# Where four modulation units of each layer are loaded, multiplied and turned

## The chip, the cores and the metric

The kernel runs on one core of one Trainium2 chip. The metric is the device time of one launch in microseconds (us); the times below are medians over runs. The profile and its trace are of one further execution of the same program.

## The reference, cut to what matters

The kernel computes one inference step of a two-layer backbone on 640 tokens (128 context, 512 latent), D_MODEL = 1024, in float32. What matters here is where the modulation vector `mod` is made and where each sixth of it is used:

```python
mod_ctx = (jax.nn.silu(c_ctx) @ w_ada[l] + b_ada[l])[None, None, :]   # w_ada[l]: 1024 x 6144
mod_lat = (jax.nn.silu(c) @ w_ada[l] + b_ada[l])[:, None, :]
...
def trunk_layer(x, mod, p, lam_init, rope, ctx):
    shift_m, scale_m, gate_m, shift_f, scale_f, gate_f = jnp.split(mod, 6, axis=-1)
    h = rms_norm(x, p['norm_mix']) * (1.0 + scale_m) + shift_m
    mix, own_ctx = token_mixers(h, p, lam_init, rope, ctx)
    x = x + gate_m * mix
    h = rms_norm(x, p['norm_ffn']) * (1.0 + scale_f) + shift_f
    x = x + gate_f * conv_ffn(h, p)
    return x, own_ctx
```

`token_mixers` holds three attentions (A differential, B latent, C grouped-query), each projected, gated by a sigmoid of its own 1024 columns of the input projection, summed, and multiplied by `w_o`. `conv_ffn` multiplies by `w_up`, applies a width-3 convolution and a gated product, and multiplies by `w_down`. The last sixth of the modulation, `gate_f`, is first read when the output of `w_down` is added to x.

## The kernel before, in words

Activations lie in SBUF with features on partitions: `xT` (x, eight tiles of 128 features by 640 tokens), and `hhi`/`hlo`, a high and a low part of the normed input. Every float32 weight is also split, on ScalarE into `whi` (line 1443) and on VectorE into `wlo` (line 1765), and every product is three matmuls (high by high, high by low, low by high). Weights arrive in units of 1 MB in `raw`, which has two slots; a split takes half a unit (a sub) and writes one of two sub buffers.

`build_plan()` writes out one list of steps, and every engine walks this same list and emits those steps that concern it. So the order in each engine's queue is the order of the list. `unit` is a load (SyncE's queue, `load_unit`), `split` the two halves of the weight split, `gate_quarter` a quarter of a gate tile's matmuls (line 1169, 12 matmuls), `gate` a whole gate tile (line 1147). `prefetch(ahead)` puts loads and splits into the list ahead of the products that need them. A load into a slot waits until the slot's former content has been used: for ordinary weights until the last split (`lo_ready`), for a modulation unit until its matmuls (`ada_summed`).

A modulation unit is 256 of the 6144 columns of `w_ada`, so a layer has 24. Step `ada` (line 1076) multiplies it straight from its `raw` slot: eight matmuls of 32 output partitions by 256 columns, into the upper half of PSUM bank 6. `ada_row` (VectorE, line 1730) copies the sums to `ada_rows`, and the `ada_turn` of that unit (line 1086: two products of a 128x128 tile with two columns), which the list holds one unit later, adds the four row groups and turns them into feature columns, kept in the low columns of bank 6. All users of bank 6 wait in `bank6_free()` for `pair3_read` (its readers, `ada_row` among them), `sums_read` and `mod_ready`. `mod` (VectorE, lines 1699 and 1703) then adds the bias and forms the scales.

The first eight units of layer 0 are made at the start of the program. The other 16, and the first eight of layer 1, are made in layer 0, four of them around the attention of branch C; in layer 1 the 16 that are left are made, again four around attention C. There the fill of the attention is, in order: one `ada`, eight quarters, one `ada`, eight quarters, two `ada`. `attention()` spreads its fill over 20 cycles by costs (`QUARTER` 1.8, `ADA_COST` 1.4). In a cycle TensorE computes scores of one block of 128 queries (line 1299), transposes the probabilities of the block before (1311) and multiplies the one before that by the values (1338); VectorE takes maxima (1839), reciprocals and products; ScalarE takes exponentials (1575); a new score waits until the exponentials of the one before are done.

After attention C come the last `ada_turn`, `mod`, and `branch(2)`: two gate tiles, four products with `w_branch_c`. Then `ffn()`: four units of `w_o` (step `wo`), the second norm, the `w_up` and `w_down` loops. The second norm is the steps `norm` (ten 128x1 records at line 1103 sum the squares, VectorE reads them at 1734, GpSimd takes the power at 2020, VectorE makes five diagonals at 1689), `spread` (line 1095) and `apply` (ScalarE 1432, VectorE 1748 and 1754). It cannot begin until the last `wo` output has been added to `xT`, squared and summed.

## Time and profile before

| | |
|---|---|
| median of 3 runs | 2800.79 us (2800.14 to 2802.28) |
| profiled execution, its own time | 2795.99 us |
| its span, first to last instruction | 2794.2 us |
| mean granted TensorE clock | 0.956 of full |
| TensorE / VectorE / ScalarE / GpSimd busy | 91% / 50% / 36% / 15% of the span |
| attention C, first score to last values | 699.7 to 807.7 us (layer 0), 2066.8 to 2172.4 us (layer 1) |
| last `w_o` matmul to first `w_up` matmul | 924.8 to 942.9 us (layer 0), 2289.4 to 2307.6 us (layer 1) |

Busy time counts computing instructions only. A stretch in which TensorE idles is read in the timeline: the bracket at the end of a row is the engine's idle time before the row and the instruction that ended it. PEclk is the granted TensorE clock as a share of full speed (2.4 GHz); the records show it at 1.00 or 0.50 (1.2 GHz).

### The profile page before, as it was taken

To read this page: it belongs to the slowest core of one execution; us is meant where nothing else is said; L and a number is where in the kernel's file an instruction comes from. 1 tells how busy PE (TensorE), PEld (TensorE's weight loads), DVE (VectorE), ACT (ScalarE), POOL (GpSimd) and SP (SyncE) were. 2 spreads that over 40 slices of the span, in tenths; PEclk is the share of its full clock that TensorE was granted. 3 is DMA by queue.
4 is the path that set the end of the run, shared out by engine and by line. 5 is a ranking of instruction groups with operands and counts; after the bars stand their busy time and mean duration, and the time that the engine had idled before them with its cause. 6 is when DMAs were issued, how large, how long until landed. Compare 5 with 4: busy or idle time off the path is not lost.

```text
span 2794.2 us, 42894 instructions
## 1 busy us (share of the span) xinstructions
PE 2546.8 (91%) x17075; PEld 2298.6 (82%) x17075; DVE 1399.7 (50%) x2386; ACT 1001.0 (36%) x1721; POOL 405.5 (15%) x362
## 2 busy tenths in 40 slices
PE   6989989988989799999988899898989889999999
PEld 4768976677779799999976688666967789999998
DVE  3665256644645444334445753575357445442453
ACT  4343144423432444123242532453235225421332
POOL 0400030123002022012004000220220201210220
PEclk8999999999999899999999999999999899999999
DMA  6201213322212122232222112222210221222222
GB/s 220 82 25 46 81 62 126 119 71 78 69 46 76 46 75 68 71 85 72 59 77 63 35 61 67 67 76 80 65 61 31 76 76 46 75 72 79 75 59 85
DMA packets 252830, 202.75 MB, mean 73 GB/s; under 512 B 9876, under 2 KB 235910, under 8 KB 252678
## 3 DMA queue, kind: packets, MB, share of 16 engines
q1 hardware_dynamic: 245574, 197.67, 23.2%
q10 hardware_dynamic: 7104, 2.95, 0.4%
q8 instruction: 108, 1.77, 0.3%
q14 instruction: 44, 0.36, 0.0%
HBM read 196.50 MB, written 4.10 MB: 72 GB/s over the span
## 4 chain that ended last, share of the span: by engine, by line
PE 76%; issue 8%; DVE 7%; ACT 6%; POOL 2%; DMA 0%; POOLq 0%; ACTq 0%; DVEq 0%; SPq 0%
PE ps L1147 44%; PE ps L1299 5%; PE ps L1169 5%; PE ps L1311 3%; PE ps L1132 3%; PE ps L1134 3%; PE ps L1133 3%; PE ps L1338 3%; ACT prob L1575 2%; PE ps L1076 1%; PE ps L1242 1%; DVE wlo L1765 1%; PE ps L1259 1%; ACT hf L1432 1%; PE ps L1086 1%
## 5 line engine op out<-in xcount | busy, mean ns | idle before, releaser
L1765 DVE TENSOR_TENSOR wlo<-raw,whi 128x1024 fp32r<-128x1024 f32 (+4 forms) x288 | 359.8, 1250 | 546.1 <-ACT whi L1443 545.3
L1147 PE MATMUL ps<-hhi,whi 128*128 128x320 f32 x2048 | 479.2, 316 | 28.1 <-DVE hlo L1748 13.3
L1147 PE MATMUL ps<-hlo,whi 128*128 128x320 f32 x2048 | 474.4, 313 | 0.0
L1147 PE MATMUL ps<-hhi,wlo 128*128 128x320 f32 x2048 | 473.5, 313 | 0.0
L1443 ACT ACTIVATE whi<-raw 128x1024 fp32r<-128x1024 f32 (+4 forms) x288 | 281.2, 978 | 393.7 <-PE ps L1147 282.5
L1147 PEld LDWEIGHTS ps<-hhi,whi 128*128 128x128 f32 x2048 | 348.6, 192 | 37.9 <-issue 28.4
L1147 PEld LDWEIGHTS ps<-hlo,whi 128*128 128x128 f32 x2048 | 350.0, 192 | 0.0
L1147 PEld LDWEIGHTS ps<-hhi,wlo 128*128 128x128 f32 x2048 | 349.6, 191 | 0.0
L1839 DVE TENSOR_REDUCE negmax<-ps 128x1 f32<-128x640 f32 x192 | 152.1, 821 | 132.6 <-PE ps L1299 132.6
L2040 POOL TENSOR_TENSOR rstd<-smean,mhalf 128x4 f32<-128x4 f32 (+3 forms) x96 | 117.1, 1223 | 612.8 <-DVE smean L1815 612.5
L1132 PE MATMUL ps<-whi,hhi 128*128 128x512 f32 (+2 forms) x480 | 180.7, 376 | 12.2 <-issue 5.7
L1585 ACT ACTIVATE probT<-ps 128x512 f32<-128x512 f32 (+1 forms) x172 | 88.3, 513 | 255.9 <-PE ps L1311 255.9
L1134 PE MATMUL ps<-whi,hlo 128*128 128x512 f32 (+2 forms) x480 | 178.1, 371 | 0.0
L1133 PE MATMUL ps<-wlo,hhi 128*128 128x512 f32 (+2 forms) x480 | 178.0, 371 | 0.0
L2064 POOL TENSOR_TENSOR va<-va,vg 128x640 f32<-128x640 f32 x44 | 74.7, 1698 | 649.8 <-ACT vg L1641 649.8
L1147 PE MATMUL ps<-ahi,whi 128*128 128x320 f32 x704 | 161.2, 310 | 4.5 <-DVE wlo L1765 3.9
L1575 ACT ACTIVATE prob<-ps,negmax 128x640 f32<-128x640 f32 x192 | 150.5, 792 | 34.3 <-DVE negmax L1839 34.1
L1147 PE MATMUL ps<-ahi,wlo 128*128 128x320 f32 x704 | 160.6, 309 | 0.0
L1147 PE MATMUL ps<-alo,whi 128*128 128x320 f32 x704 | 160.5, 309 | 0.0
L1169 PE MATMUL ps<-hhi,whi 128*128 128x320 f32 x384 | 138.2, 360 | 8.5 <-DVE wlo L1765 8.5
L1311 PEld LDWEIGHTS ps<-ident,prob 128*128 128x128 f32 x840 | 91.8, 141 | 58.9 <-issue 24.0
L1311 PE MATMUL ps<-ident,prob 128*128 128x128 f32 x840 | 127.6, 282 | 12.4 <-DVE prob L1870 8.4
(208 smaller groups left out, 4237.9 us busy)
## 6 DMA issues: line engine op xcount, KB each, us to landing
raw<-in_w_up SPq DMA_DIRECT2D x88, 512.0 KB, 4.9
raw<-in_w_in SPq DMA_DIRECT2D x40, 1024.0 KB, 5.2
raw<-in_w_ada SPq DMA_DIRECT2D x40, 1024.0 KB, 5.2
raw<-in_w_down SPq DMA_DIRECT2D x16, 768.0 KB, 4.8
raw<-in_w_down SPq DMA_DIRECT2D x16, 640.0 KB, 4.5
adaw<-in_w_ada SPq DMA_DIRECT2D x8, 1024.0 KB, 10.5
raw<-in_w_o SPq DMA_DIRECT2D x8, 1024.0 KB, 5.1
raw<-in_w_branch_a SPq DMA_DIRECT2D x4, 1024.0 KB, 6.1
```

Of the source, the lines that this page charges most:

```text
L1132: pe.matmul(out, hhi[:, kt, c], wh, start=kt == 0, stop=False)
L1133: pe.matmul(out, hhi[:, kt, c], wl, start=False, stop=False)
L1134: mm = pe.matmul(out, hlo[:, kt, c], wh, start=False, stop=kt == KD - 1)
L1147: mm = pe.matmul(out, w[:, sub, c], m[:, kt, o:o + HALF], start=first and i == 0 and a == 0, stop=last and i == len(ks) - 1 and a == 2)
L1169: mm = pe.matmul(bank(6)[:, OFF:], w[:, s["sub"], c], m[:, kt, o:o + HALF], start=kt == a == 0, stop=kt == KD - 1 and a == 2)
L1299: mm = pe.matmul(out, qt[:, q * P:(q + 1) * P], kt[:, SEQ + c:SEQ + c + HALF], start=True, stop=True)
L1311: mm = pe.transpose(bank(bk)[:, i * P:(i + 1) * P], src, ident[:, :])
L1443: act.activation(dst(whi), src, ACT.Copy).then_inc(S["hi_ready"], 1)
L1575: act.activation(prob[:, slot + m, :], run(m), ACT.Exp, bias=negmax[:, at], accum_out=den[:, at])\
L1765: dve.tensor_tensor(dst(wlo), src, dst(whi).bitcast(F32), ALU.subtract).then_inc(S["lo_ready"], 1)
L1839: dve.tensor_reduce(negmax[:, slot + m:slot + m + 1], run(m), AX.X, ALU.max, negate=True)\
L2040: pool.tensor_tensor(rstd[:, par, 0:heads], smean[:, par, 0:heads], mhalf[:, 0:heads], ALU.pow)\
```

## The change

Units 20 to 23 of each layer, whose 1024 columns are `gate_f`, leave the common row of units. The others are made in the order of a list, `ADA_ORDER`; the fill of attention C is then the 16 quarters alone. The four units get SBUF places of their own: `adaC` over the space of `qC`, `kC` and `vC`, `adaT` behind `gatedC`. Step `load_tail` loads all four in SyncE's queue, behind the load of the first `w_o` unit and ahead of the second. In the second norm, steps `tail` multiply them on TensorE into banks 0 to 3 behind the last `w_o` matmuls and ahead of `norm`; ScalarE copies the sums back over the units' own first columns; `tail_turn` turns them on TensorE between `norm` and `spread`; `tail_mod` adds the bias on VectorE after `apply`. `down_out` gets a wait for `mod_ready`.

```diff
+ADA_TAIL = range(5 * KD // 2, 6 * KD // 2)
+ADA_ORDER = [(l + (u < ADA_FIRST // 2), u) for l in range(DEPTH)
+             for u in [*range(ADA_FIRST // 2, ADA_TAIL[0]), *range(ADA_FIRST // 2 if l + 1 < DEPTH else 0)]]
...
     def queue_ada(n):
         for _ in range(n):
-            of, u = divmod(count["ada_unit"], 3 * KD)
+            of, u = ADA_ORDER[count["ada_unit"]]
...
-                for u in (2, 4):
-                    queue_ada(1)
-                    queue_gates(2, u, 1)
-                queue_ada(2)
+                queue_gates(2, 2, 2)
                 queue_branch(2)
...
-        attention("C", range(NH), [ada_steps, quarter_gates, quarter_gates, ada_steps, quarter_gates, quarter_gates,
-                                   ada_steps, ada_steps],
+        attention("C", range(NH), [quarter_gates] * 4,
...
-        left = fm_units("wo", KD // 2, SUB, [], early=last, between=[dict(step="zero", l=l, what="wo")], l=l)
-        norm2 = [dict(step=x, which=1, l=l) for x in ("norm", "spread")]
-        norm2.append(dict(step="apply", which=1, l=l, ks=range(KD), kept=False))
+        left = fm_units("wo", KD // 2, SUB, [], early=last, between=[dict(step="zero", l=l, what="wo"), dict(step="load_tail", l=l)], l=l)
+        norm2 = [dict(step="tail", l=l, i=i) for i in range(len(ADA_TAIL))] + [dict(step="norm", which=1, l=l)]
+        norm2 += [dict(step="tail_turn", l=l, i=i, c=ada_column(u)) for i, u in enumerate(ADA_TAIL)]
+        norm2 += [dict(step="spread", which=1, l=l), dict(step="apply", which=1, l=l, ks=range(KD), kept=False),
+                  dict(step="tail_mod", l=l)]
...
+                def load_tail(s):
+                    sp.wait_ge(S["av_done"], n("av_done"))
+                    sp.wait_ge(S["lam_step"], n("lam_step"))
+                    sp.wait_ge(S["rows_turned"], n("rows_turned"))
+                    for i, u in enumerate(ADA_TAIL):
+                        sp.dma_start(tail_unit(i).rearrange("p (k c) -> p k c", k=KD),
+                                     w_ada[s["l"]:s["l"] + 1, :, u * 256:(u + 1) * 256].rearrange("l (k p) c -> p (l k) c", p=P))\
+                          .then_inc(S["tail_full"], 16)
...
+                def tail(s):
+                    i = s["i"]
+                    pe.wait_ge(S["tail_full"], n("tail_full"))
+                    pe.wait_ge(S["fm_read"], n("fm_read", -2))
+                    for k in range(KD):
+                        g = 32 * (k % 4)
+                        mm = pe.matmul(bank(i)[g:g + 32, 0:256], cpad[:, k, :], tail_unit(i)[:, k * 256:(k + 1) * 256],
+                                       start=k < 4, stop=k >= 4)
+                    mm.then_inc(S["tail_summed"], 1)
+
+                def tail_turn(s):
+                    bank6_free()
+                    pe.wait_ge(S["tail_read"], n("tail_read", s["i"] + 1 - len(ADA_TAIL)))
+                    for j in range(2):
+                        c = s["c"] + 2 * j
+                        mm = pe.matmul(bank(6)[:, c:c + 2], tail_unit(s["i"])[:, j * P:(j + 1) * P], add4[:, :],
+                                       start=True, stop=True)
+                    mm.then_inc(S["ada_done"], 1)
...
+                def tail(s):
+                    act.wait_ge(S["tail_summed"], n("tail_summed", 1))
+                    act.activation(tail_unit(s["i"])[:, 0:256], bank(s["i"])[:, 0:256], ACT.Copy).then_inc(S["tail_read"], 1)
...
+                def tail_mod(s):
+                    l, t, m = s["l"], 2 * ADA_TAIL[0], 2 * len(ADA_TAIL)
+                    c = ADA_AT + 2 * (t - ADA_FIRST)
+                    dve.wait_ge(S["ada_done"], n("ada_done"))
+                    dve.tensor_tensor(mod[:, l, t:t + m, :], bank(6)[:, c:c + 2 * m].rearrange("p (t j) -> p t j", j=2),
+                                      PT[:, l, t:t + m].unsqueeze(2).to_broadcast([P, m, 2]), ALU.add).then_inc(S["mod_ready"], 1)
...
                 def down_out(s):
                     dve.wait_ge(S["sub_done"], n("sub_done"))
+                    dve.wait_ge(S["mod_ready"], n("mod_ready"))
```

## Rows read from the trace of the kernel before

**Rows 1.** The page: busy us (share of the span) and instructions of each engine.

```profile
PE 2546.8 (91%) x17075; PEld 2298.6 (82%) x17075; DVE 1399.7 (50%) x2386; ACT 1001.0 (36%) x1721; POOL 405.5 (15%) x362
```

**Rows 2.** Windows of layer 0: length, busy us per engine, PEclk, DMA share, GB/s.

```profile
712.00:757.00 45.00, 44.56 (x396) 35.14 (x394) 30.95 (x59) 22.21 (x52) 0.00 (x0) 0.99 0.01 2
...
807.80:820.50 12.70, 3.90 (x24) 2.54 (x24) 4.48 (x10) 4.62 (x6) 0.00 (x0) 0.66 0.43 117
...
924.80:942.90 18.10, 4.73 (x15) 3.41 (x15) 9.21 (x18) 5.36 (x8) 1.17 (x1) 0.59 0.21 58
```

**Rows 3.** Timeline, end of attention C, layer 0 (start us, us, engine line op).

```profile
806.54 0.61 PE L1086 MATMUL ps<-add,ada_rows 128*128 128x2 f32 x4
806.67 0.37 SPq L980 DMA_DIRECT2D raw<-in_w_in  x1
807.08 0.66 PE L1333 MATMUL ps<-probT,vC 128*64 128x128 f32 x8
811.90 2.00 ACT L1443 ACTIVATE whi<-raw 128x1024 fp32r<-128x1024 f32 x2 [6.90 <-DMA raw<-in_w_in]
...
814.13 0.42 DVE L1730 COPY ada_rows<-ps 128x256 f32<-128x256 f32 x1
...
814.81 1.94 PE L1076 MATMUL ps<-raw,cpad 128*32 128x256 f32 x16 [7.07 <-issue]
816.68 1.01 PE L1086 MATMUL ps<-add,ada_rows 128*128 128x2 f32 x4
...
820.56 0.87 PE L1147 MATMUL ps<-hhi,whi 128*128 128x320 f32 x2 [1.27 <-DVE scale L1703]
...
825.49 0.50 PE L1147 MATMUL ps<-hhi,whi 128*128 128x320 f32 x2
```

**Rows 4.** Timeline, start of attention C, layer 0.

```profile
699.66 2.50 PE L1299 MATMUL ps<-kC,qC 64*128 64x320 f32 x8 [0.77 <-ACT PT L1401]
...
706.87 0.42 DVE L1730 COPY ada_rows<-ps 128x256 f32<-128x256 f32 x1
...
707.39 0.60 PE L1169 MATMUL ps<-hhi,whi 128*128 128x320 f32 x1 [3.42 <-DVE wlo L1765]
...
710.86 1.44 PE L1299 MATMUL ps<-kC,qC 64*128 64x320 f32 x4
```

**Rows 5.** Timeline, start and end of attention C, layer 1.

```profile
2066.81 1.35 PE L1299 MATMUL ps<-kC,qC 64*128 64x320 f32 x8 [0.69 <-ACT qC L1530]
...
2076.88 2.02 PE L1299 MATMUL ps<-kC,qC 64*128 64x320 f32 x8
...
2184.69 0.87 PE L1147 MATMUL ps<-hhi,whi 128*128 128x320 f32 x2 [0.83 <-DVE scale L1703]
```

**Rows 6.** Timeline, one full cycle, and the `ada` of cycle 11, layer 0.

```profile
716.62 1.35 PE L1299 MATMUL ps<-kC,qC 64*128 64x320 f32 x8
...
719.86 0.80 ACT L1575 ACTIVATE prob<-ps,negmax 128x640 f32<-128x640 f32 x1
...
722.29 1.35 PE L1299 MATMUL ps<-kC,qC 64*128 64x320 f32 x8
...
757.27 1.07 PE L1076 MATMUL ps<-raw,cpad 128*32 128x256 f32 x16
```

**Rows 7.** Timeline, the second norm's wait, layer 0.

```profile
931.52 2.26 PE L1103 MATMUL ps<-ones,hf 128*128 128x1 f32 x10 [6.75 <-DVE hf L1958]
...
936.48 2.47 PE L1095 MATMUL ps<-diag,ones 128*128 128x320 f32 x4 [2.70 <-DVE diag L1689]
```

**Rows 8.** `w_o` loads, the split that needs the second, and a loaded DMA window.

```profile
841.18 0.38 SPq L1001 DMA_DIRECT2D raw<-in_w_o  x1
858.74 0.37 SPq L1001 DMA_DIRECT2D raw<-in_w_o  x1
...
875.88 1.06 ACT L1443 ACTIVATE whi<-raw 128x1024 fp32r<-128x1024 f32 x1 [2.56 <-PE ps L1147]
...
10.00:20.00 10.00, 2.97 (x22) 2.31 (x20) 3.90 (x5) 9.97 (x18) 0.00 (x0) 0.83 1.08 386
```

More of the change, by code:

```diff
@@ L170, in first_chunk @@
     def first_chunk():
-        count.update(ada=ADA_FIRST // 2, ada_turn=ADA_FIRST // 2)
         add("load_first", us=(0, 4))
@@ L203, in ada_turn @@
         if count["ada"] > count["ada_turn"]:
-            add("ada_turn", c=ada_column(count["ada_turn"]), u=None)
+            add("ada_turn", c=ada_column(*ADA_ORDER[count["ada_turn"]][::-1]), u=None)
             count["ada_turn"] += 1
@@ L538, in build_plan @@
         ffn(l)
-    assert count["gate"] == 3 * KD * DEPTH and count["ada"] == 3 * KD * DEPTH
+    assert count["gate"] == 3 * KD * DEPTH and count["ada"] == len(ADA_ORDER)
     look_back(plan)
@@ L613, in signals @@
         return dict(ada_done=1)
+    if k == "load_tail":
+        return dict(tail_full=16 * len(ADA_TAIL))
+    if k == "tail":
+        return dict(tail_summed=1, tail_read=1)
+    if k == "tail_turn":
+        return dict(ada_done=1)
+    if k == "tail_mod":
+        return dict(mod_ready=1)
     if k == "mod":
@@ L1360, in obcast @@
                         mm.then_inc(S["obc_done"], 1)
-                do = dict(params=params, ada=ada, ada_turn=ada_turn, norm=norm, spread=spread, tm=tm, gate_part=gate_part, gate_quarter=gate_quarter, gate=gate, branch=branch, wo=wo, up=up, down=down,
+                do = dict(params=params, tail=tail, tail_turn=tail_turn, ada=ada, ada_turn=ada_turn, norm=norm, spread=spread, tm=tm, gate_part=gate_part, gate_quarter=gate_quarter, gate=gate, branch=branch, wo=wo, up=up, down=down,
                           turnc=turnc, turn=turn, upmm=upmm, score=score, turnp=turnp, values=values, ostat=ostat,
@@ L1644, in up_out2 @@
                        .then_inc(S["ahi_ready"], 1)
-                do = dict(params=params, gains=gains_, norm=norm, wo_out=wo_out, down_out=down_out, apply=apply, split=split, acc=acc, tick=tick, turn=turn, turnc=turnc, gate=gate, gate_quarter=gate_quarter, expo=expo,
+                do = dict(params=params, tail=tail, gains=gains_, norm=norm, wo_out=wo_out, down_out=down_out, apply=apply, split=split, acc=acc, tick=tick, turn=turn, turnc=turnc, gate=gate, gate_quarter=gate_quarter, expo=expo,
                           turnp=turnp, osq=osq, osplit=osplit, msplit=msplit, up_out=up_out,
@@ L1994, in up_out @@
                         ins.then_inc(S["fm_read"], 1)
-                do = dict(gains=gains_, ada_row=ada_row, mod=modulation, mod_pair=mod_pair, keep=keep, norm=norm, apply=apply, split=split, tick=tick, flush=flush, score=score,
+                do = dict(gains=gains_, ada_row=ada_row, tail_mod=tail_mod, mod=modulation, mod_pair=mod_pair, keep=keep, norm=norm, apply=apply, split=split, tick=tick, flush=flush, score=score,
                           soft=soft, turnp=turnp, values=values, ostat=ostat, obcast=obcast, osplit=osplit, merge=merge,
```

20 lines of the change are left out of this document (10 added, 10 removed).

## The prediction, made before the changed kernel was run

> **What bounds the kernel now.** I read the page first: TensorE is busy for 91% of the span, and no other engine for more than 50% [rows 1]. So the change matters where TensorE is full and loses work, or where it idles and the cause goes. The second view was the table of windows over the stages that the change touches [rows 2]. Inside attention C TensorE is busy for 44.56 of 45.00 us; between the last values and the first gate tile 12.70 us hold 3.90 us of work; and the second norm has 18.10 us with 4.73. The reader is to see a full stretch and two holes, with a mean clock of 0.66 and 0.59 in them. The timeline then says what each hole is, and shows a third at the start of the attention.
>
> At the end of attention C a modulation unit holds its slot of `raw` until its matmuls are through. Only then, at 806.67, is the next weight load issued; its split begins at 811.90; VectorE makes `wlo` and, queued behind it, copies `ada_rows` at 814.13; and the last unit's matmuls, which need that copy, start at 814.81 after 7.07 us of idle TensorE [rows 3]. Then follow its own turn, a second copy and turn, and `mod`, so that the gate tile starts at 820.56. At the start of attention C it is the same in small: `ada_rows` is copied at 706.87 behind a split, and the first quarter starts at 707.39 after 3.42 us of idle [rows 4]. Layer 1 shows both too [rows 5].
>
> **The end of attention C.** The values end at 807.08 + 0.66 = 807.74 and the gate tile starts at 820.56: 12.8 us [rows 3]. After the change one turn is left (four records, 0.61 us in this group's first row), then `mod` and the start of the gate tile. From the last turn to `mod` and to the gate tile the rows give an upper bound: 816.68 to 820.56 is 3.9 us with two turns and a copy between; taking out one turn of 1.0, one copy of 0.4 and its two hand-overs of about 0.3 leaves 2.0 us. So 10.8 us go. In layer 1 the values end at 2172.4 and the gate tile starts at 2184.69 [rows 5]: 12.3 us; `mod` has half the instructions there, so about 1.6 us stay and 10.7 go. What is late next? The gate tile's weights: their load no longer follows an `ada` but a gate unit whose last split is done early in the attention, so they lie there about 90 us before. The idle time that is left is one hand-over chain of 1.3 us. The clock is a second term. The pair of products at 820.56 takes 0.87 us and the one at 825.49 takes 0.50 [rows 3]: the gate tile runs for 4.9 us at the low level of 1.2 GHz. What the level costs is read from the same work at both: the first score takes 2.50 us at the low level and 1.35 at the full one [rows 4, 6], a unit's matmuls 1.94 and 1.07 [rows 3, 6], so a ratio of 0.55. So 4.9 us at the low level cost 2.2 us more than at full; layer 1's gate tile begins at the low level too [rows 5], and for it I take half, 1.1. With a gap of 1.3 us instead of 7.07 I count both as gained; the other bound is nothing.
>
> **The start of attention C.** Before, the first score starts at 699.66 and the second at 710.86 [rows 4]. Afterwards TensorE has the score (2.50 us, low clock) and a quarter, which at the low clock takes 3.3 us (707.39 to 710.86 less the hand-over to the score), to 705.5; the second score also waits for the exponentials, 4.04 us behind the first score's start in a full cycle [rows 6], some 5 us here. So it starts at 705.5 and 5.4 us go. In layer 1 the first score takes 1.35 us at full clock, the quarter 3.3 by the ratio, 1.85, the exponentials end at 4.04: the second score starts at 2070.9 instead of 2076.88 [rows 5], 6.0 us earlier, and takes 1.35 us instead of 2.02: 6.7 in all. For clock that comes back earlier in layer 0 I add 0.4; bounds 0 and 1.3.
>
> **Within attention C.** The other two units in the fill cost TensorE 1.07 us of matmuls [rows 6] and 0.61 of turn [rows 3] each, overlapping slightly: 1.6 each, 3.2 a layer. The 16 quarters now spread over 20 cycles at 1.44 of cost each, so about every fifth cycle has none. A cycle with a quarter takes 722.29 - 716.62 = 5.67 us; without its quarter, 1.85 and a hand-over, TensorE needs 3.75, but the second exponential ends at 719.86 + 0.80, 4.04 us in, and the next score follows at about 4.1 [rows 6]. Three such cycles idle 0.4 us each: 1.2 us back, up to 3 if a split of 1.05 us on ScalarE falls into them. VectorE is busy for 30.95 of 45.00 us [rows 2] and loses four copies of 0.42 a layer, worth nothing by themselves.
>
> **Sum of what goes.** Layer 0: 10.8 + 2.2 + 5.4 + 0.4 + 3.2 - 1.2 = 20.8. Layer 1: 10.7 + 1.1 + 6.7 + 3.2 - 1.2 = 20.5. Together 41.3 us.
>
> **What is added in the second norm.** TensorE idles 6.75 us before `norm` [rows 7], from 924.77. Four units of 1.07 us are 4.3 us, to 929.1; the squares that `norm` waits for are ready at 931.5, so 2.4 us are spare and the matmuls cost nothing. If the squares' chain were not there they would cost their 4.3. ScalarE's four copies of 128x256 are nearest to VectorE's copy of the same shape, 0.42 us [rows 3], 1.7 us in all; ScalarE is busy for 5.36 of these 18.10 us [rows 2], and its other work there is the squares and a split ahead of them and `apply` behind. They are done near 931 and free. The four turns must fit between the read of the sums and `spread`: TensorE idles 2.70 us there [rows 7], of which I put 0.2 down to the read. At full clock four turns of 0.61 are 2.4: nothing. At the low level a turn takes 1.01 [rows 3], four 4.0 us: 1.5 us more per layer. And the clock itself: `norm` takes 2.26 us and `spread` 2.47 at the low level [rows 7]. If the tail's matmuls hold the clock up, both shrink by the ratio 0.55, by 1.0 and 1.1 us, 2.1 in all. So a layer's norm lies between -2.1 and +1.5. The idle stretch that remains is 2.4 us instead of 6.75, which speaks for the first end; but the clock is lowered elsewhere without so long a gap (the score at 699.66 is at the low level after an idle of 0.77 [rows 4]). I take 0, between the two.
>
> The Trainium skill weighs in here: "TensorE: Matmul & The Clock Gate", Part 1, has the clock follow how busy the array was shortly before. By that rule the filled wait keeps full clock and the norm gives back 2.1 us a layer; by the row of the low score behind a short gap it need not. The trace has no norm with a filled wait, so it can't decide; the sum keeps 0.
>
> `tail_mod` is one small VectorE instruction (the copy of 0.42 us [rows 3] bounds it) behind `apply`, while TensorE has the first `w_up` tile; nothing. The new wait in `down_out` is for it, a whole `w_up` loop later; nothing.
>
> **The four loads.** Each is 1 MB and is issued in SyncE's queue between the first and second `w_o` load, at 0.37 us of issue each. Its three waits are for things done in attention C. The second `w_o` load goes out at 858.74, 17.6 us behind the first, and its first split runs at 875.88 when a sub buffer is free, not when the data comes [rows 8]. With many loads queued the DMA moves 386 GB/s [rows 8], so 4.2 MB take 10.9 us and are through before the second `w_o` load is even issued. The second load's spare time is 17.1 us less the 5.2 that a lone 1 MB takes to land (806.67 to 811.90 [rows 3]): 11.9 us. If the tails came one by one at the 5.2 us that such a load takes alone, they would end 26 us behind the first load's issue; the second `w_o` unit would land at 31.2, still before 34.7, when it is needed. Cost 0 from both ends.
>
> **The rivals.** (a) The clock stays full through the second norm: 4.2 us less, 2755.3. For it: matmuls where there was idle time; against it: the low score above. (b) The turns run at the low clock and delay `spread`, 3.0 us: 2762.5. For it: before, the clock is low in that place in both layers. (c) The end of attention C changes its cause but does not go: the split chain of the last gate unit, now behind ScalarE's four `ohi` copies, or the clock, keeps 5 to 7 us a layer, 2770 to 2773. Against it: the weights are loaded early and the first sub's split has a free buffer. (d) The attention is bound by the softmax chain more often than every fifth cycle, by up to 1.8 us more a layer and with no gain from the removed units, 3.2: 10 us, 2769.5. Against it: TensorE is 99% busy there. (e) Slower: the tails hold up the second `w_o` load. It would need 11.9 us of delay before anything is lost and 20.6 more a layer before the gain is gone, so 32.5 us; the tails would have to end 50 us behind the first `w_o` load instead of 16, four times as slow, before it decides; at five times a layer loses 30 us, and the result is 2820. Nothing in the rows moves 1 MB that slowly. (f) The holes have another cause than the units and nothing changes: 2801. Against it: the copy of `ada_rows` stands in both chains.
>
> **How the numbers follow.** The profiled execution took 2795.99 us, 1.8 outside its span; less 41.3 it is 2754.7. The median of the runs shown is 4.8 above it, 2800.79; less 41.3 it is 2759.5, my forecast. Chances: the forecast as summed, within 2 us either way, 0.42; (a) 0.20; (b) 0.18; (c) 0.09; (d) 0.07; (e) 0.02; (f) 0.02. The low end takes (a) with the unused clock and cycle terms' good ends (another 3.5): 2752. The high end takes (b) and (d) together, or (c) alone: 2773. Faster by over 0.2% (5.6 us, about what a measurement of this kernel can tell) 0.96, within it 0.02, slower 0.02.
>
> **What would show it.** No load of a gate unit near the end of attention C; the gate tile 2 us behind the last values in layer 0 at full clock; the second score 6 us behind the first in layer 0 and 4 in layer 1; the attention shorter from first score to last values by 7.8 us in layer 0 and 8.7 in layer 1; four tail loads landed before 875.88 less the shift; `norm` starting 6.75 us behind the last `w_o` matmul as now. Wrong it would be through a clock that drops in the 1.3 us gap, through a gate unit that still loads late, or through a `norm` that starts later than now.

## The result and the profile after

| | before | changed |
|---|---|---|
| median | 2800.47 us (2798.59 to 2802.28, 4 runs) | 2763.18 us (2760.51 to 2764.07, 4 runs) |
| profiled execution | 2795.99 us | 2764.07 us |
| its span, mean granted clock | 2794.2 us, 0.956 | 2762.3 us, 0.958 |

The ratio is 0.9868, with a 95% interval of 0.9853 to 0.9883: 37.3 us less between the medians, where 41.3 were forecast, and the time is 3.7 us above the forecast 2759.5. The same program once more, on another chip with its own runs of the kernel before (E0 below), gave 2762.41 against 2803.12 us, 40.7 us less.

Totals of the page hardly move. Its first part for the changed kernel, to be laid beside [rows 1]:

```profile
PE 2547.7 (92%) x17075; PEld 2299.2 (83%) x17075; DVE 1396.7 (51%) x2380; ACT 1002.8 (36%) x1729; POOL 405.5 (15%) x362
```

TensorE has the same 17075 matmul records and nearly the same busy time, 2547 us; VectorE has lost eight copies and gained two small instructions, ScalarE has gained eight copies. The totals hide two opposite things, so the gain has to be found in stretches. From the first score of attention C to the first `w_up` matmul, both layers together, TensorE's idle time falls by 32.3 us and its busy time by 9.5 (425.7 to 416.2 us, with the same number of matmul records), because the granted clock there is higher: 0.92 in both layers before, 0.96 and 0.97 after. Everywhere else its busy time is 10.4 us longer in this trace; what that is stands in the section on the sum. The timeline of the changed kernel at the end of attention C in layer 0, answering to [rows 3]:

```profile
802.51 0.66 PE L1372 MATMUL ps<-probT,vC 128*64 128x128 f32 x8
...
803.11 0.61 PE L1104 MATMUL ps<-add,ada_rows 128*128 128x2 f32 x4
...
803.75 0.21 DVE L1742 TENSOR_TENSOR mod<-ps,PT 128x48 f32<-128x48 f32 x1
...
804.96 0.53 PE L1186 MATMUL ps<-hhi,whi 128*128 128x320 f32 x2 [1.25 <-DVE scale L1746]
```

The last values end at 803.17 and the gate tile (line 1186) starts 1.8 us later. One turn and `mod` stand between; no load, no split, no copy. Its first pair takes 0.53 us instead of 0.87: the granted clock is the full one, 2.4 GHz, after a gap of 1.25 us.

The start of attention C in layer 0, timeline of the changed kernel, answering to [rows 4]:

```profile
704.58 2.37 PE L1338 MATMUL ps<-kC,qC 64*128 64x320 f32 x8 [0.77 <-ACT PT L1440]
...
706.88 0.63 PE L1208 MATMUL ps<-hhi,whi 128*128 128x320 f32 x1
...
708.63 0.79 ACT L1618 ACTIVATE prob<-ps,negmax 128x640 f32<-128x640 f32 x1
...
709.56 1.35 PE L1338 MATMUL ps<-kC,qC 64*128 64x320 f32 x8
```

The second score now waits only for the second exponential (708.63 + 0.79 = 709.42); it starts 4.98 us behind the first instead of 11.20. The split that the first quarter needs has moved too: before, its `wlo` is made at 705.73, behind the exponentials of the first score; in the changed kernel the last `wlo` ahead of that quarter is made at 701.74, before the first score. And the second norm's wait in layer 0 of the changed kernel, first TensorE's timeline, answering to [rows 7], then ScalarE's:

```profile
908.39 1.93 PE L1115 MATMUL ps<-adaC,cpad 128*32 128x256 f32 x32
910.14 1.91 PE L1115 MATMUL ps<-adaT,cpad 128*32 128x256 f32 x32
915.21 1.25 PE L1142 MATMUL ps<-ones,hf 128*128 128x1 f32 x10 [3.16 <-DVE hf L2008]
916.76 1.84 PE L1125 MATMUL ps<-add,adaC 128*128 128x2 f32 x8 [0.30 <-issue]
918.46 1.84 PE L1125 MATMUL ps<-add,adaT 128*128 128x2 f32 x8
920.17 2.48 PE L1134 MATMUL ps<-diag,ones 128*128 128x320 f32 x4
```

```profile
912.05 0.64 ACT L1452 ACTIVATE adaC<-ps 128x256 f32<-128x256 f32 x2
912.58 0.66 ACT L1452 ACTIVATE adaT<-ps 128x256 f32<-128x256 f32 x2
```

The reader is to see that the four units fit (3.7 us, then 3.16 of idle time are still left ahead of `norm`), that `norm` starts at its old distance (6.74 us behind the last `w_o` matmul), that it takes 1.25 us instead of 2.26, and that the four turns take 3.4 us behind it and end where `spread` begins: 3.71 us behind `norm` instead of 2.70.

The same landmarks, read from the timelines of both kernels in both layers (each is a difference of two starts or ends in the trace; us):

| stretch | before, layer 0 / 1 | changed, layer 0 / 1 | difference, both layers | forecast |
|---|---|---|---|---|
| first score to second | 11.20 / 10.07 | 4.98 / 4.76 | -11.5 | -12.5 |
| second score to end of last values | 96.88 / 95.52 | 93.61 / 93.58 | -5.2 | -4.0 |
| last values to gate tile | 12.82 / 12.29 | 1.79 / 1.39 | -21.9 | -21.5 |
| gate tile to last `w_o` matmul | 104.22 / 104.76 | 103.51 / 101.96 | -3.5 | -3.3 |
| last `w_o` matmul to first `w_up` matmul | 18.12 / 18.12 | 18.13 / 18.50 | +0.4 | 0 |
| sum | | | -41.8 | -41.3 |

### The profile page after: what moved, and what is told of

Its sections match the earlier page's. It is cut to its first block, busy times and chain, and to the rows that moved or that the text cites. A ratio compares the mean times of both kernels' runs of the same rounds, so it can differ in the third digit from the quotient of the medians.

```text
span 2762.3 us, 42924 instructions
## 1 busy us (share of the span) xinstructions
PE 2547.7 (92%) x17075; PEld 2299.2 (83%) x17075; DVE 1396.7 (51%) x2380; ACT 1002.8 (36%) x1729; POOL 405.5 (15%) x362
## 4 chain that ended last, share of the span: by engine, by line
PE 81%; DVE 7%; ACT 6%; issue 3%; POOL 2%; DMA 1%; POOLq 0%; SPq 0%; ACTq 0%; DVEq 0%
PE ps L1186 49%; PE ps L1338 5%; PE ps L1208 5%; PE ps L1350 3%; PE ps L1171 3%; PE ps L1173 3%; PE ps L1172 3%; PE ps L1377 3%; ACT prob L1618 2%; PE ps L1094 1%; PE ps L1281 1%; DVE wlo L1815 1%; PE ps L1298 1%; ACT hf L1475 1%; POOL tmps L2084 1%
## 5 line engine op out<-in xcount | busy, mean ns | idle before, releaser
L1186 PEld LDWEIGHTS ps<-hhi,whi 128*128 128x128 f32 x2048 | 347.3, 191 | 38.5 <-issue 28.3
```

The costliest lines, as they stand in the source:

```text
L1186: mm = pe.matmul(out, w[:, sub, c], m[:, kt, o:o + HALF], start=first and i == 0 and a == 0, stop=last and i == len(ks) - 1 and a == 2)
```

## The experiments

Each ratio is to the kernel before on the same chip: E0, E1, E4 and E6 ran on one chip (kernel before there: 2803.12 us), E2, E3 and E5 on another (2801.68), E7 and E8 on a third (2803.26).

**E0: the changed kernel again.**

> The changed kernel again, beside the kernels run with it. Both theories: 2763 us and a ratio of 0.987 to the kernel before. Its trace shows whether attention B's second half, unchanged by the change but 4.6 us longer in the first trace after it (layer 0), is longer again (then the change costs there) or not (then the low clock at its start is chance).

Measured: 2762.41 us (2760.06 to 2767.35), ratio 0.9854 [0.983, 0.9878]. From the first score of attention C to the first `w_up` matmul it takes 222.24 and 221.10 us, where the first trace has 222.02 and 220.19 and the kernel before 243.24 and 240.76. These stretches repeat to within 1 us. The second half of attention B in layer 0, first to last score, took 47.2 us as in the kernel before (47.1), where the first trace of the changed kernel had 50.2. By the test that was set, its lengthening in the first trace was chance; the granted clock there was 0.88 in that trace and 0.95 and 0.94 in the other two.

**E1: the tails' work left out.** Loads, matmuls, copies, turns and `tail_mod` of the four units are gone, and the last residual uses the columns of another sixth of the modulation, so that part of the computation is left out.

```diff
-        left = fm_units("wo", KD // 2, SUB, [], early=last, between=[dict(step="zero", l=l, what="wo"), dict(step="load_tail", l=l)], l=l)
-        norm2 = [dict(step="tail", l=l, i=i) for i in range(len(ADA_TAIL))] + [dict(step="norm", which=1, l=l)]
-        norm2 += [dict(step="tail_turn", l=l, i=i, c=ada_column(u)) for i, u in enumerate(ADA_TAIL)]
-        norm2 += [dict(step="spread", which=1, l=l), dict(step="apply", which=1, l=l, ks=range(KD), kept=False),
-                  dict(step="tail_mod", l=l)]
+        left = fm_units("wo", KD // 2, SUB, [], early=last, between=[dict(step="zero", l=l, what="wo")], l=l)
+        norm2 = [dict(step="norm", which=1, l=l)]
+        norm2 += [dict(step="spread", which=1, l=l), dict(step="apply", which=1, l=l, ks=range(KD), kept=False)]
...
-                    residual(n.turn * 2 + s["a"], 2 * s["s"], 5 * KD, s["l"])
+                    residual(n.turn * 2 + s["a"], 2 * s["s"], 4 * KD, s["l"])
```

> The changed kernel with the four tail units' loads, matmuls, copies, turns and sum left out; the MLP's residual is scaled by scale_f in place of gate_f. Theory: their work lies in TensorE's idle time, norm's start and spread's start keep their distance from the last w_o matmul within 0.5 us, and the time is that of the changed kernel, 2763, within 2 us. Rival: the 7 us of tail work per layer is paid somewhere, and without it the time is 2750.

Measured: 2761.58 us (2756.67 to 2762.14), ratio 0.9855 [0.9832, 0.9878], against 0.9854 for E0 beside it, as the theory had it; the rival's 2750 is out. The second norm of this run, TensorE in layer 0:

```profile
912.35 2.27 PE L1140 MATMUL ps<-ones,hf 128*128 128x1 f32 x10 [6.75 <-DVE hf L2006]
917.32 2.47 PE L1132 MATMUL ps<-diag,ones 128*128 128x320 f32 x4 [2.70 <-DVE diag L1730]
923.73 0.87 PE L1184 MATMUL ps<-hhi,whi 128*128 128x320 f32 x2 [3.95 <-DVE hlo L1796]
```

These are the numbers of [rows 7] again: 6.75, 2.27, 2.70, 2.47. The stretch from the last `w_o` matmul to the first `w_up` matmul is 18.12 us in both layers; with the tails it is 18.13 and 18.50 (E0: 18.26 and 18.62). So a layer's 4 MB of loads, 32 matmuls (64 records), four copies and eight small products (16 records) cost 0.0 to 0.5 us where they now stand.

**E2: the kernel before, with only the order of its fill changed**, so that no unit stands at the end of attention C: two units, eight quarters, two units, eight quarters.

```diff
-                for u in (2, 4):
-                    queue_ada(1)
-                    queue_gates(2, u, 1)
                 queue_ada(2)
+                queue_gates(2, 2, 1)
+                queue_ada(2)
+                queue_gates(2, 4, 1)
...
-        attention("C", range(NH), [ada_steps, quarter_gates, quarter_gates, ada_steps, quarter_gates, quarter_gates,
-                                   ada_steps, ada_steps],
+        attention("C", range(NH), [ada_steps, ada_steps, quarter_gates, quarter_gates, ada_steps, ada_steps,
+                                   quarter_gates, quarter_gates],
```

> The kernel before with attention C's fill in another order alone: two units, eight quarters, two units, eight quarters, so that no unit stands at its end. Theory: the hole at the end of attention C (10.8 and 10.7 us, and 2.2 and 1.1 of clock) comes from the last units holding a slot and from the copy behind the split; without them there it goes, and the hole at the start and the units' own 1.7 us each stay: some 22 us less, 2778 (2775 to 2785). Rival: the gain is due to the units being out of attention C; the order alone gives under 5 us, 2796 or more.

Measured: 2815.41 us (2812.78 to 2816.92), ratio 1.0055 [1.0037, 1.0073]: slower than the kernel before. The theory's 2778 was wrong; the time lies where the rival put it (2796 or more), but the rival had no slowdown either. The hole at the end did go: the gate tile starts 1.81 and 1.38 us behind the last values. But one has come in the middle of the attention, and the one at its start has grown: the second score comes 14.84 and 13.61 us behind the first instead of 11.20 and 10.07. The timeline of E2 in layer 0, around the first pair of units and at the second:

```profile
704.46 1.59 PE L1076 MATMUL ps<-raw,cpad 128*32 128x256 f32 x16
...
706.11 0.38 SPq L980 DMA_DIRECT2D raw<-in_w_in  x1
...
711.24 2.00 ACT L1443 ACTIVATE whi<-raw 128x1024 fp32r<-128x1024 f32 x2 [4.16 <-DMA raw<-in_w_in]
712.32 1.23 DVE L1765 TENSOR_TENSOR wlo<-raw,whi 128x1024 fp32r<-128x1024 f32 x1 [4.46 <-ACT whi L1443]
713.47 0.42 DVE L1730 COPY ada_rows<-ps 128x256 f32<-128x256 f32 x1
...
714.09 1.93 PE L1076 MATMUL ps<-raw,cpad 128*32 128x256 f32 x16 [7.52 <-issue]
...
779.59 1.94 PE L1076 MATMUL ps<-raw,cpad 128*32 128x256 f32 x16 [7.58 <-issue]
```

It is the chain of [rows 3] link by link: the unit's matmuls give the slot free, the load goes out at 706.11, its split runs at 711.24 when it lands, the copy of `ada_rows` stands behind `wlo` in VectorE's queue, and the next unit, which needs bank 6 read, comes after 7.5 us of idle TensorE. The copy's data is there from 706.05 on, and VectorE is idle for 4.46 us with the copy waiting behind `wlo`. (The Trainium skill, "TensorE: Matmul & The Clock Gate", in the table at its head, lists VectorE's queue as strictly first in, first out; the trace agrees, by this row.) So the hole belongs to a pair of units with a load between them, not to the end of the attention. Before there was one pair, at the end; E2 has two, and each makes its hole.

**E3: the kernel before, with the copy put ahead of the load and split.**

```diff
             add("ada", slot=ada_ready.pop(0), bank=6)
-            prefetch(1)
             ada_turn()
             add("ada_row", u=None)
+            prefetch(1)
```

> The kernel before with the copy of each unit's sums put into the list ahead of the next load and split, the units where they were. Theory: the copy behind the split makes the hole at the start of attention C, which shrinks by 3 us and some clock, and about half of that at the end, where the gate tile then waits for its weights (load at 806.7, ready at 814.3) and no longer for two more turns: 4 + 6 us a layer, and some in attention B: 2776 to 2780. Rival: the late load makes both holes, and the copy's place gives under 5 us.

Measured: 2797.53 us (2795.5 to 2801.71), ratio 0.9992 [0.9981, 1.0002]: no difference clear of noise. The theory was wrong, and the rival held (under 5 us). The timeline of E3 at the end of attention C in layer 0:

```profile
808.66 1.07 PE L1076 MATMUL ps<-raw,cpad 128*32 128x256 f32 x16 [0.15 <-issue]
809.66 0.61 PE L1086 MATMUL ps<-add,ada_rows 128*128 128x2 f32 x4
...
812.83 2.00 ACT L1443 ACTIVATE whi<-raw 128x1024 fp32r<-128x1024 f32 x2 [7.07 <-DMA raw<-in_w_in]
813.92 1.23 DVE L1765 TENSOR_TENSOR wlo<-raw,whi 128x1024 fp32r<-128x1024 f32 x1 [5.48 <-ACT whi L1443]
...
816.53 0.42 DVE L1730 COPY ada_rows<-ps 128x256 f32<-128x256 f32 x1
817.00 1.01 PE L1086 MATMUL ps<-add,ada_rows 128*128 128x2 f32 x4 [6.74 <-DVE ada_rows L1730]
...
819.28 0.87 PE L1147 MATMUL ps<-hhi,whi 128*128 128x320 f32 x2 [1.27 <-DVE scale L1703]
```

The last unit has indeed moved up, to 0.15 us behind its forerunner's turn. But the late load is still there, and now the last unit's own copy (816.53) waits behind its split; the idle time has only gone one step further, ahead of that unit's turn. The hole is 10.78 and 10.60 us instead of 12.82 and 12.29: the copy's place is worth about 2 us a layer by itself. At the start of the attention nothing changed (11.20 us to the second score), because the split ahead of the copy there comes from the `prefetch(2)` at the head of `ada()`.

**E7: the kernel before, with places of their own for the last two units of attention C.** They are loaded two thirds into the attention into `adaT` behind `gatedC`, and still multiplied in the attention's last cycles. No work leaves the attention.

```diff
+    def own_steps():
+
+        def one():
+            i = count["ada"] % 2
+            add("ada", slot=10 + i, bank=6)
+            ada_turn()
+            add("ada_row", u=None)
+            count["ada"] += 1
+        return [(ADA_COST, one)]
...
-                queue_ada(2)
+                own[:] = [divmod(count["ada_unit"] + i, 3 * KD) for i in range(2)]
+                count["ada_unit"] += 2
...
-                                   ada_steps, ada_steps],
-                  {-8: [dict(kind="gains", of=at["l"] + 1)]} if more else {})
+                                   own_steps, own_steps],
+                  {-7: [dict(kind="load_own", units=list(own))], **({-8: [dict(kind="gains", of=at["l"] + 1)]} if more else {})})
...
+                def load_own(s):
+                    sp.wait_ge(S["av_done"], n("av_done"))
...
+                    for i, (of, u) in enumerate(s["units"]):
+                        sp.dma_start(adaT[:, i, :].rearrange("p (k c) -> p k c", k=KD),
```

> The kernel before with one thing of the change alone: the last two modulation units of attention C get a place of their own behind gatedC and are loaded there once the next layer's small parameters are through (two thirds into the attention), but they are still multiplied and turned in the attention's fill, in the same last cycles. All work stays; only the two loads no longer wait for a slot of raw, and the gate unit's load and split no longer stand between them. Theory now (the end hole is made by the gate unit's load, which waits for the slot that a modulation unit holds, and by the copy of ada_rows behind that load's split): the idle 7.07 us ahead of the last unit goes, and from the last values to the gate tile there remain one copy, one turn and mod, some 3.5 us instead of 12.8 and 12.3. That is about 9 us a layer, 18 in all: near 2783, ratio 0.9935. Rival (the hole is the work of the two units and their turns itself, which only leaving the attention can remove): the hole shrinks by the late load's idle only in part, 9 to 11 us are left, and the time is 2796 or more. The start of the attention, 11.2 us to the second score, stays as it was under both.

Measured: 2783.78 us (2782.55 to 2785.21), ratio 0.9928 [0.9915, 0.994], as the theory had it. The timeline of E7 at the end of attention C in layer 0:

```profile
808.95 0.66 PE L1357 MATMUL ps<-probT,vC 128*64 128x128 f32 x8
809.81 1.07 PE L1100 MATMUL ps<-adaT,cpad 128*32 128x256 f32 x16 [0.20 <-issue]
810.81 0.61 PE L1110 MATMUL ps<-add,ada_rows 128*128 128x2 f32 x4
812.00 0.61 PE L1110 MATMUL ps<-add,ada_rows 128*128 128x2 f32 x4 [0.58 <-DVE ada_rows L1754]
813.88 0.87 PE L1171 MATMUL ps<-hhi,whi 128*128 128x320 f32 x2 [1.27 <-DVE scale L1727]
```

The last unit follows the values at once, the copy takes its 0.42 us, and the gate tile comes 4.27 us behind the last values (3.88 in layer 1). The place alone took 8.5 of the 11.0 us that the change took out of this hole in layer 0, and 8.4 of 10.9 in layer 1. That is the late load, its split and the copy's wait behind it, together. The first score to the second is unchanged (11.20 and 10.06). The gate tile of layer 0 is back at the low clock (0.87 us for its first pair); that of layer 1 is at the full one (0.53).

**E5: the kernel before, with the four units moved into attention B** through the common slots.

```diff
-            queue_ada(5 + 4 * more)
+            queue_ada(7 + 4 * more)
...
-                for u in (2, 4):
-                    queue_ada(1)
-                    queue_gates(2, u, 1)
-                queue_ada(2)
+                queue_gates(2, 2, 2)
...
-            attention("B", range(2 * half, 2 * half + 2), [ada_steps] * (8 if more else 4))
+            attention("B", range(2 * half, 2 * half + 2), [ada_steps] * (10 if more else 6))
...
-        attention("C", range(NH), [ada_steps, quarter_gates, quarter_gates, ada_steps, quarter_gates, quarter_gates,
-                                   ada_steps, ada_steps],
+        attention("C", range(NH), [quarter_gates] * 4,
```

> The kernel before with the four units of each layer moved from attention C into attention B's fill, still through the two slots; nothing in the second norm. Theory: attention C gains what it gains in the changed kernel (38 us in all), attention B pays 1.68 us of TensorE for each of eight units, 13.4 us: 2776. Rival: attention B has room beside its softmax chain and takes them for nothing: 2762.

Measured: 2773.34 us (2772.18 to 2775.13), ratio 0.9906 [0.9884, 0.9927]. From the first score of C to the first `w_up` matmul it gains what the change gains, 21.3 and 20.2 us. The medians give only 28.3 of these 41.5; the missing 13 us are close to the 13.4 that the theory put down for attention B, where the units now are, but they were not followed there instruction by instruction. The theory's 2776 held to 3 us, and the rival, 2762, is out. So the emptied attention C is worth some 20 us a layer whoever takes the units, and the second norm's wait is the cheaper place for them: ratios of 0.9906 against 0.9854 and 0.9868, which is 11 to 15 us, lie between a full place and an idle one.

**E4: the changed kernel with the tails' turns ahead of `norm`.**

```diff
-        norm2 = [dict(step="tail", l=l, i=i) for i in range(len(ADA_TAIL))] + [dict(step="norm", which=1, l=l)]
+        norm2 = [dict(step="tail", l=l, i=i) for i in range(len(ADA_TAIL))]
         norm2 += [dict(step="tail_turn", l=l, i=i, c=ada_column(u)) for i, u in enumerate(ADA_TAIL)]
-        norm2 += [dict(step="spread", which=1, l=l), dict(step="apply", which=1, l=l, ks=range(KD), kept=False),
+        norm2 += [dict(step="norm", which=1, l=l), dict(step="spread", which=1, l=l), dict(step="apply", which=1, l=l, ks=range(KD), kept=False),
...
                     bank6_free()
+                    pe.wait_ge(S["fm_read"], n("fm_read"))
```

> The changed kernel with the four tail turns ahead of norm instead of between norm and spread. Theory: they fit into the 3.2 us that TensorE still idles before norm, and spread no longer waits for them: spread starts 2.5 us behind the end of norm instead of 3.7, so 1.0 us in layer 0 and 1.2 in layer 1, and up to 1.1 more a layer if the clock is then still full at spread: 2759 to 2761. Rival: the turns wait for ScalarE's copies, which run behind a split, and norm starts up to 1 us later: 2763 or more.

Measured: 2760.27 us (2755.56 to 2764.02), ratio 0.9844 [0.9818, 0.987], inside the theory's 2759 to 2761. The second norm of E4, TensorE in layer 0:

```profile
912.42 1.02 PE L1126 MATMUL ps<-add,adaC 128*128 128x2 f32 x8 [0.51 <-ACT adaC L1453]
913.31 1.03 PE L1126 MATMUL ps<-add,adaT 128*128 128x2 f32 x8
915.08 1.25 PE L1143 MATMUL ps<-ones,hf 128*128 128x1 f32 x10 [0.74 <-DVE hf L2009]
919.02 2.47 PE L1135 MATMUL ps<-diag,ones 128*128 128x320 f32 x4 [2.70 <-DVE diag L1733]
```

The turns now take 1.9 us at full clock in time that was idle, `norm` is not later, and `spread` is back at 2.70 us behind it. The norm's stretch is 17.11 and 17.95 us instead of 18.26 and 18.62 in E0. This is 1.8 us in the trace; the medians differ by 2.1, within their scatter, so the gain is shown by the trace and not by the times.

**E6 and E8: E4 and E3's edit together**, on the changed kernel; the same program twice.

> As the kernel with the turns ahead of norm, and in every modulation unit of the common row the copy of its sums is put into the list ahead of the next load and split. Theory: wherever a unit's copy stood behind a split that waited for a load (the ends of attentions A and B), TensorE gets back 3 us or more: 2750. Rival: those holes are set by the weights' load alone, and nothing changes against the kernel with the turns ahead of norm.

> The same program as the earlier run with both the tails' turns ahead of norm and the copy of ada_rows ahead of the next prefetch, once more and beside other programs, to see how firm its time is. If its 2757.1 us was real, it comes out again between 2754 and 2760, ratio 0.982 to 0.986; if it was a lucky draw of where the low clock falls, it comes out at the changed kernel's 2761 to 2763.

Measured: E6 2757.11 us (2753.9 to 2757.4), ratio 0.9838 [0.9815, 0.9862]; E8 2754.53 us (2750.29 to 2759.88), ratio 0.9824 [0.9807, 0.984]. So the time repeated, inside the range set for E8, and E6's theory, 2750, was too bold. Beside E0 on the same chip E6 is 5.3 us faster, beside E4 3.2. The changed stretch explains a part of it: 220.96 + 220.26 us in E6 and 220.02 + 220.27 in E8 against 222.24 + 221.10 in E0, 2 to 3 us. Ahead of attention C in layer 0 TensorE idles 89.5 us in both, where it idles 90.2 in E4 and 91.6 in E0, so at most 2 us of idle time have gone there; the larger difference, 605.3 and 609.8 us busy against 611.5 and 612.7, is clock and differs as much between E6 and E8. Where the rest comes from stays open. It is the fastest version that was run.

## Why the prediction was right, and where its terms were off

**The sum.** The two stretches lost 21.2 and 20.6 us in the traces; 20.8 and 20.5 were forecast. The medians lost 37.3 and, in E0, 40.7; the spans of the two traces lost only 31.9. What is missing between 41.8 and 31.9 lies in stages that the change doesn't touch: attention C of layer 0 begins 4.9 us later in the trace (704.58 against 699.66), and from layer 0's first `w_up` matmul to layer 1's attention C it takes 1128.9 us where it took 1123.9. The windows of this second stretch, before and then changed, say what the difference is (length, busy us of TensorE, its weight loads, VectorE, ScalarE and GpSimd, PEclk, DMA):

```profile
942.90:2066.81 1123.91, 1037.18 (x6724) 944.95 (x6725) 560.36 (x958) 408.58 (x690) 186.14 (x167) 0.97 0.22 66
926.60:2055.50 1128.90, 1042.85 (x6725) 948.89 (x6725) 560.31 (x959) 408.44 (x690) 186.06 (x167) 0.96 0.22 66
```

The work is the same and VectorE and ScalarE take as long as before. TensorE is busy for 5.7 us more at a lower mean clock, and it idles no longer (86.1 against 86.7 us). Ahead of attention C in layer 0 it is the same: 4.7 of the 4.9 us are busy time of the same 3923 matmul records. So the missing 10 us are time at the low clock, not a wait. In the second stretch they are not the change's: E7, whose program there is that of before, took 1128.2 us, E2 and E3 1128.4 and 1128.8, but E1, with the changed order, took 1124.0, and E0 1131.3. The one trace of before was short there, as its own time says, 2795.99 us against a median of 2800.47. Ahead of attention C in layer 0 the two groups of traces differ a little: it begins at 699.7 to 702.1 us in before, E2, E3 and E7, and at 701.8 to 704.6 in the changed kernel, E0, E1 and E4. Whether a small part of the 3.7 us between forecast and median belongs to the change can't be told from these runs. The median lies outside the 2 us either way for which the forecast had its chance of 0.42. By its number it stands nearest to rival (b), 2762.5, but not by its cause, as the second norm shows below.

**The end of attention C.** 11.0 and 10.9 us against 10.8 and 10.7: right in size. The prediction read the chain from the late load to the copy, and E7 shows that the chain as a whole (late load, split, copy behind it) is 8.5 of the 11 us; E3 shows that the copy's place behind the split is some 2 us when it alone is changed. It tied the hole to the end of the attention; E2 shows that it is tied to two units in a row. A gate unit beside a unit does no such harm, two units with a load between do. Only the change, E5 and E7 take the pair's slot away, and only they take most of the hole away without losing elsewhere in C.

**The clock of the gate tile.** 2.2 + 1.1 forecast, 0.7 + 2.8 measured from the gate tile to the last `w_o` matmul. The gate tile does start at full clock in both layers (0.53 us for the first pair; 0.87 in both before), as the prediction had it, and its terms were about right: before, the low level held for 4.9 us of it in layer 0 and 2.8 in layer 1 (until 2187.5), which at the ratio 0.55 is 2.2 and 1.3 us. Another spell of low clock lies over them, in the `w_o` stage, and it costs 1.5 us each time. The changed kernel has it in layer 0 and not in layer 1, behind the same wait of 1.85 us (timeline, layer 0, then layer 1):

```profile
850.37 0.54 PE L1186 MATMUL ps<-hhi,whi 128*128 128x320 f32 x2 [1.85 <-DVE gatedC L1977]
...
852.21 0.74 PE L1186 MATMUL ps<-hhi,wlo 128*128 128x320 f32 x2
...
2200.63 0.53 PE L1186 MATMUL ps<-hhi,whi 128*128 128x320 f32 x2 [1.85 <-DVE gatedC L1977]
```

In layer 0 the pairs take 0.74 us from 851.7 to 854.9 and then 0.46 again; in layer 1 they stay at 0.46. The kernel before has the spell in layer 1 only (granted clock 0.83 from 2227 to 2237). So 2.2 - 1.5 and 1.3 + 1.5 give the 0.7 and 2.8 that were measured, and the sum came out by luck: the two spells cancel. Of the 12 such stretches in the traces of the changed kernel, E0, E1, E4, E6 and E8, eight take 103.5 us (one spell), three 102.0 (none) and one 105.0 (two), with no edit that goes with it. The second spell of the last one, in layer 0 of E4, begins 0.4 us into the gate tile: the drop of the clock at the 1.3 us gap, which the prediction named as a sign against itself, came once in 12.

**The start of attention C.** 6.2 and 5.3 us against 5.4 + 0.4 and 6.7. The forecast 6.7 holds 0.7 for a shorter second score, which in the table falls into the second row; with the same bounds the forecast of the first two rows is -11.8 and -4.7, against -11.5 and -5.2. In layer 0 the clock came back in the middle of the quarter, which the prediction had put wholly at the low level: the second score came at 4.98 us and not at 5.8. In layer 1 the first quarter ran at the low level in part: the first score takes 1.62 us where 1.35 were assumed, and the quarter behind it starts with 0.47 us a matmul where the full level has 0.31. So the second score came at 4.76 and not at 4.04. In E0, E1, E4, E6 and E8 it came at 4.01 or 4.02: the forecast names the commoner of two cases that occur. No run separates here what the unit's own work costs from what the late split costs; E3 shows that the copy's place costs nothing there, though the prediction put the start down to the same chain as the end.

**Within attention C.** 3.3 and 1.9 us against 2.0 each. The window that answers to the first of [rows 2], TensorE in the changed kernel, has 43.63 busy us of 45.00 where before had 44.56:

```profile
712.00:757.00 45.00, 43.63 (x392) 34.73 (x392) 32.48 (x64) 23.11 (x55) 0.00 (x0) 1.00 0.09 28
```

TensorE idles 1.4 us in it instead of 0.4, as the cycles without a quarter should make it. Over the whole stretch its busy time falls by 3.8 and 3.3 us, where 3.2 was forecast for the two units, and its idle time rises by 0.5 and 1.4, where 1.2 was forecast. The softmax chain does not take more than that: rival (d) is out.

**The second norm.** Forecast 0 between -2.1 and +1.5; measured 0.0 and +0.4. The 0 was the middle of two bounds and not a mechanism, and that it held is luck: parts of both bounds happened at once and cancelled. The tails' matmuls kept the full clock to the end of `norm` in layer 0, which takes 1.25 us instead of 2.26, and into it in layer 1 (1.61): at most half of rival (a). Behind it the clock fell to 1.2 GHz, the turns took 3.4 us and `spread` came 1.0 us later: rival (b), 1.0 where it had 1.5. Timeline of the changed kernel in layer 1:

```profile
2263.94 1.61 PE L1142 MATMUL ps<-ones,hf 128*128 128x1 f32 x10 [3.16 <-DVE hf L2008]
2265.86 1.84 PE L1125 MATMUL ps<-add,adaC 128*128 128x2 f32 x8 [0.30 <-issue]
2267.55 1.85 PE L1125 MATMUL ps<-add,adaT 128*128 128x2 f32 x8
2269.26 2.48 PE L1134 MATMUL ps<-diag,ones 128*128 128x320 f32 x4
```

"TensorE: Matmul & The Clock Gate" of the Trainium skill, Part 1, has the clock follow how busy the array was shortly before; the traces agree as far as `norm`: behind a filled wait (changed kernel, E0, E4, E6, E8) it takes 1.25 to 2.09 us, behind an empty one (before and E1) 2.26 or 2.27. But the 2.1 us a layer that a full clock up to `spread` would give back did not come, not even in E4, where TensorE idles only 0.74 us ahead of `norm`, then 2.70 behind it, and `spread` still takes 2.47. Four units take 3.7 us, not 4.3: back to back they cost 0.92 us each. ScalarE's four copies take 1.2 us, not 1.7.

Against rival (a) the prediction held that the score at 699.66 is at the low clock after only 0.77 us of idle time. That reading took the last gap alone. In the 4.2 us ahead of this score TensorE idles three times, 3.0 us in all (timeline of the kernel before; the third is the 0.77):

```profile
696.96 0.65 PE L1242 MATMUL ps<-ident,stage 128*128 128x128 f32 x4 [1.50 <-DVE stage L1780]
698.35 0.28 PE L1046 MATMUL ps<-ident,vB 109*128 109x109 f32 x1 [0.73 <-issue]
```

So that row does not show a clock that falls behind a short gap; the spells in the `w_o` stage and in E4 above come nearer to it, behind waits of 1.85 and 1.25 us.

**The four loads.** 0, as forecast. The queue of SyncE in the changed kernel, timeline of the `w_o` stage:

```profile
823.34 0.38 SPq L1019 DMA_DIRECT2D raw<-in_w_o  x1
823.85 1.56 SPq L967 DMA_DIRECT2D adaC<-in_w_ada  x2
...
828.79 2.58 SPq L967 DMA_DIRECT2D adaT<-in_w_ada  x1
...
840.90 0.36 SPq L1019 DMA_DIRECT2D raw<-in_w_o  x1
...
859.57 1.06 ACT L1486 ACTIVATE whi<-raw 128x1024 fp32r<-128x1024 f32 x1 [4.12 <-PE ps L1186]
```

The second `w_o` load goes out 17.6 us behind the first, as in [rows 8], and the split that needs it is released by TensorE and not by the DMA. One thing was not foreseen: the third tail load holds the queue from 825.46 for 3.29 us and the fourth, issued at 828.79, for 2.58 us, so an issue can take more than its 0.37 us when loads are queued. The queue is then idle from 831.4 to 840.9, and by 840 to 841 the DMA share is 0.00, so all four have landed before the second `w_o` load goes out. Nothing comes of it, and rival (e) had no part.

**Rivals (c) and (f)** are out: the hole did not change its cause, it went.

## What to carry to other kernels

When work that keeps a buffer until its matmuls are done stands twice in a row, look at what the first one's release triggers: here a 1 MB load of 5 us, a split queued behind it, and a copy queued behind the split made 7 to 7.5 us of idle TensorE a pair, and neither another order of the fill nor an earlier place of the copy removed it, while a place of its own did. Before a unit is moved, ask separately what its place costs and what its work costs: of 12.8 us at the end of the attention 8.5 were the place. Compare stretches, and then look whether the rest of the program took the same time: 10 us of this trace pair were clock in stretches that the change leaves alone. And a wait that must stay is a cheaper home for such work than a full attention (E5), best if its small follow-up steps are put into the same wait too, and not into the next and shorter one (E4).

## What the runs showed of the hardware beside this

- The clock fell behind a wait that was mostly filled. In layer 0 of E4 TensorE was idle for 0.51 and 0.74 us in the 6.8 us ahead of `norm`, ran `norm` at 2.4 GHz (1.25 us), idled for 2.70 us and had `spread` at 1.2 GHz (2.47 us).
- The same wait can be followed by either level. Behind 1.85 us of idle time in the `w_o` stage the changed kernel fell to 1.2 GHz about 1 us into the next matmuls in layer 0 and stayed at 2.4 GHz in layer 1. Behind 1.25 us the gate tile of layer 0 stayed at 2.4 GHz in the changed kernel, and in E4 the clock fell 0.4 us into it.
- Eight matmuls into 32 output partitions by 256 columns cost 1.07 us alone and 0.92 in a row of 32 (3.7 us).
- Single executions differ by up to 7 us in a stretch in which their programs hardly differ (1123.9 us in the kernel before to 1131.3 in E0, from the first `w_up` matmul of layer 0 to attention C of layer 1). The idle time is nearly the same in both (86.7 and 85.4 us); TensorE's busy time is not (1037.2 and 1045.9 us, for the same matmuls), and the mean granted clock is 0.97 and 0.96. What brings on the spells at 1.2 GHz was not tested.
